# Routes of an expert layer: paired one-hots, row gathers that follow the quads, and route stores in four pieces

## What is computed

```
for l in range(2):
    h = rmsnorm(x, norm1_g[l]) * (1 + sc1) + sh1
    x = x + g1 * hybrid_mixer(h, ...)          # y = sum_i sigmoid(gate_i(h)) * (branch_i @ w_branch[i])
    h = rmsnorm(x, norm2_g[l]) * (1 + sc2) + sh2
    x = x + g2 * peer_ffn(h, ...)

def peer_ffn(h, w_q, sub_keys, u_tab, v_tab):  # 128 x 128 experts, 8 heads, top 16 of each
    experts, g = top16(product keys)           # 128 (expert, share) pairs for each token
    a = gelu(h . u_tab[experts]) * g
    return sum over experts of a * v_tab[experts]
```

## Time and profile before

| what | value |
|---|---|
| median of three runs | 4460.01 us (4444.33 to 4460.23) |
| the profiled execution, its own time | 4453.37 us |
| span of its core | 4451.4 us |
| TensorE, matmul busy | 3973.7 us, 89% |
| VectorE busy | 2640.4 us, 59% |
| ScalarE busy | 1511.7 us, 34% |
| GpSimd busy | 1276.2 us, 29% |
| mean granted TensorE clock | 0.954 |
| DMA | 906.71 MB, mean 204 GB/s |

### The profile page before, as it was taken

The page is one execution under the profiler, slowest core; times in us unless marked ns, Lnnn a source line. Parts: engine busy times, 40 slices in busy tenths (PEclk is TensorE's granted clock), DMA queues, the critical chain, the costliest instruction groups (busy, mean ns, idle before and its releaser), DMA issues.

```text
span 4451.4 us, 61311 instructions
## 1 busy us (share of the span) xinstructions
PE 3973.7 (89%) x18070; PEld 2992.1 (67%) x18070; DVE 2640.4 (59%) x5662; ACT 1511.7 (34%) x2428; POOL 1276.2 (29%) x884
## 2 busy tenths in 40 slices
PE   5888999799998989999869889997999988899998
PEld 2334455399998987777624344653999888777776
DVE  3443323246997957777634432331579988577776
ACT  3224333233443333333332333432334433333332
POOL 0000000046865652222100000000468655422221
PEclk9898999999999999999989899998999999999999
DMA  4341112134788899998634311122357888888885
GB/s 167 114 146 44 56 50 93 69 136 162 262 299 306 339 334 328 327 335 319 217 117 149 104 50 54 62 90 76 136 186 257 315 301 323 323 323 318 321 323 217
DMA packets 340821, 906.71 MB, mean 204 GB/s; under 512 B 28688, under 2 KB 160016, under 8 KB 337168
## 3 DMA queue, kind: packets, MB, share of 16 engines
q1 hardware_dynamic: 215824, 497.43, 31.7%
q0 software_dynamic: 84480, 306.22, 18.6%
q10 hardware_dynamic: 40320, 100.68, 5.9%
HBM read 788.87 MB, written 115.34 MB: 203 GB/s over the span
## 4 chain that ended last, share of the span: by engine, by line
PE 44%; DMA 17%; issue 15%; DVE 15%; POOL 4%; ACT 3%; DVEq 1%; POOLq 0%; SPq 0%; ACTq 0%; PEldq 0%
DMA W<-tab_v 14%; PE bank L683 13%; PE bank L753 7%; PE bank L672 4%; PE bank L674 4%; PE bank L673 4%; DVE u_lo L1950 3%; PE bank L809 2%; PE bank L780 2%; POOL gathered_rows L1431 2%; DMA gathered_rows<-u_rows,arena 2%; PE bank L739 1%; DVE gathered_rows L1820 1%; DVE arena L1860 1%; PE bank L723 1%
## 5 line engine op out<-in xcount | busy, mean ns | idle before, releaser
L1423 POOL TENSOR_TENSOR u_lo<-W,u_hi 128x1024 fp32r<-128x1024 f32 x272 | 688.7, 2533 | 1154.2 <-ACT u_hi L1256 1152.1
L672 PE MATMUL bank<-h_hi,u_hi 128*128 128x384 f32 (+1 forms) x2176 | 765.9, 352 | 48.5 <-POOL u_lo L1423 46.1
L673 PE MATMUL bank<-h_lo,u_hi 128*128 128x384 f32 (+1 forms) x2176 | 744.8, 342 | 0.0
L674 PE MATMUL bank<-h_hi,u_lo 128*128 128x384 f32 (+1 forms) x2176 | 744.6, 342 | 0.0
L672 PE MATMUL bank<-u_hi,a_hi 128*128 128x512 f32 x1536 | 608.7, 396 | 74.3 <-DVE a_lo L1954 74.1
L674 PE MATMUL bank<-u_hi,a_lo 128*128 128x512 f32 x1536 | 604.3, 393 | 0.0
L673 PE MATMUL bank<-u_lo,a_hi 128*128 128x512 f32 x1536 | 604.3, 393 | 0.0
L1339 ACT ACTIVATE u_hi<-W 128x1024 fp32r<-128x1024 f32 x256 | 272.5, 1064 | 756.3 <-DMA W<-tab_v 388.2
L672 PEld LDWEIGHTS bank<-h_hi,u_hi 128*128 128x128 f32 x2176 | 417.3, 192 | 59.7 <-issue 37.0
L673 PEld LDWEIGHTS bank<-h_lo,u_hi 128*128 128x128 f32 x2176 | 417.2, 192 | 5.4
L674 PEld LDWEIGHTS bank<-h_hi,u_lo 128*128 128x128 f32 x2176 | 415.3, 191 | 5.4
(11 more groups left out here) (191 smaller groups left out, 5774.5 us busy)
## 6 DMA issues: line engine op xcount, KB each, us to landing
W<-tab_u SPq DMA_DIRECT2D x256, 512.0 KB, 3.7
W<-tab_v SPq DMA_DIRECT2D x256, 512.0 KB, 9.5
W<-stream SPq DMA_DIRECT2D x206, 512.0 KB, 3.7
act_scratch<-act_out ACTq DMA_DIRECT2D x256, 192.0 KB
route_scratch<-arena ACTq DMA_DIRECT2D x24, 2048.0 KB, 11.1
act_in<-act_scratch SPq DMA_DIRECT2D x64, 768.0 KB, 5.7
g_cur<-route_scratch SPq DMA_DIRECT2D x64, 768.0 KB, 10.2
gate_raw<-gate_tiles POOLq DMA_DIRECT2D x48, 512.0 KB, 4.1
```

Source lines behind the costliest of these rows:

```text
L672: mm(out, w[0], a[0], start=first, stop=False)
L673: mm(out, w[0], a[1], start=False, stop=False)
L674: return mm(out, w[1], a[0], start=False, stop=last)
L1423: nc.gpsimd.tensor_tensor(u_parts[1][:, b, :], raw, u_parts[0][:, b, :].bitcast(F32), ALU.subtract).then_inc(col_lo.sem, 1)
```

## The change

Five edits:
- The two one-hots of a quad lie beside each other in memory and are made by one tensor_tensor of 1024 elements; the share is multiplied in by a second tensor_tensor of 512 elements, in place, after the row product, from a copy of the shares in bank 3. The waits for the picks and the two copies of the shares stand at the head of the stage and at q = 2 of its first step.
- The gathers follow a list, GATHERED: 28 rows plus the quads of the columns so far, at most four in one column, and two a column in "rest".
- A group's store goes out as four transfers of 1024 columns, two in a column of the loop (all that is left at the last), and the semaphore's counts are four times as high.
- The gate products of a turn come directly after its scores, ahead of turn, output and the parts beside.
- Waits on the store's semaphore follow the new counts.

```diff
@@ -311,6 +311,7 @@
 
         at[0] = shared
         route = [carve(128 * TOKENS, [128, TOKENS]) for _ in range(2)]
+        onehots = arena[:, at[0]:at[0] + 4096].rearrange("p (s b t i) -> p s b t i", s=2, b=4, t=4)
         cand = carve(HEADS * 256, [HEADS, 256])
         onehot16 = carve(HEADS * 256, [HEADS * 16, 16])
         pickT = carve(3 * DENSE, [3, DENSE])
@@ -444,12 +445,17 @@
             QUADS[n] = list(range(first, first + width))
             first += width
         assert first == Q, first
+        GATHERED, ahead = [], 24 + 4
+        for c in range(2 * COLUMNS["route"] + COLUMNS["rest"]):
+            ahead += len(QUADS[c % COLUMNS["route"]]) if c < 2 * COLUMNS["route"] else 2
+            GATHERED.append(min(ahead, SPARSE + 6))
         iota_placed = sem("iota_placed")
+        shares_placed = sem("shares_placed")
         onehots_i = signal("onehots_i", {"route": Q})
         onehots_g = signal("onehots_g", {"route": Q})
         route_product = signal("route_product", {"route": Q})
         route_copied = signal("route_copied", {"route": Q})
-        route_stored = [Signal(sem(f"route_stored{b}"), {"route": 48}, credit=16) for b in range(2)]
+        route_stored = [Signal(sem(f"route_stored{b}"), {"route": 192}, credit=16) for b in range(2)]
 
         h_hi_done = sem("h_hi_done")
         h_lo_done = sem("h_lo_done")
@@ -645,7 +651,7 @@
 
 
                 for b in range(2):
-                    sp.wait_ge(route_stored[b].sem, route_stored[b].at("route", layer, STEPS["route"] - 1, 48))
+                    sp.wait_ge(route_stored[b].sem, route_stored[b].at("route", layer, STEPS["route"] - 1, 192))
                     sp.wait_ge(act_stored[b].sem, act_stored[b].at("rest", layer, 0, 0))
                     sp.sem_inc(held, 1)
                 load_down(0, first=True)
@@ -813,6 +819,9 @@
                 for u in range(len(units) + 3):
                     if u < len(units):
                         scores(u)
+                    if stage in GATE_WORK:
+                        for i, k in gate_products(stage, u):
+                            gate_product(stage, layer, step, i, k, bool(beside))
                     if 2 <= u <= len(units) + 1:
                         turn(u - 2)
                         if stage == "swa":
@@ -821,9 +830,6 @@
                         output(u - 3)
                     for part in [p for after, p in beside if after == u]:
                         part()
-                    if stage in GATE_WORK:
-                        for i, k in gate_products(stage, u):
-                            gate_product(stage, layer, step, i, k, bool(beside))
                     if stage == "swa" and u == 0 and not beside:
 
                         load_wait("swa", layer, step, 0)
@@ -1298,6 +1304,8 @@
                     columns("select", 0)
                     with act.Fori(1, TT) as step:
                         columns("select", step, former=step - 1)
+                    unsent = []
+
                     def copy_routes(step, n):
 
                         for q in QUADS[n]:
@@ -1305,15 +1313,23 @@
                             b = group % 2
                             act.wait_ge(route_product.sem, route_product.at("route", layer, step, q + 1))
                             if q % 8 == 0:
-                                act.wait_ge(route_stored[b].sem, route_stored[b].at("route", layer, step, 16 * (group // 2)))
+                                act.wait_ge(route_stored[b].sem, route_stored[b].at("route", layer, step, 64 * (group // 2)))
                             t0 = q % 8 * 4
                             fn(route[b][:, :, t0:t0 + 4], PS[q % 3][:].rearrange("p (t j) -> p j t", t=4), ACT.Copy
                                ).then_inc(route_copied.sem, 1)
                             if q % 8 == 7:
                                 act.wait_ge(route_copied.sem, route_copied.at("route", layer, step, q + 1))
-                                act.dma_start(route_dram[:, ds(step * 6 + group, 1), :].rearrange("p a n -> p (a n)"),
-                                              route[b].rearrange("p j t -> p (j t)")
-                                              ).then_inc(route_stored[b].sem, 16)
+                                unsent.extend((group, part) for part in range(4))
+
+                    def send_routes(step, n):
+
+                        for _ in range(len(unsent) if n == COLUMNS["route"] - 1 else min(2, len(unsent))):
+                            group, part = unsent.pop(0)
+                            b = group % 2
+                            act.dma_start(route_dram[:, ds(step * 6 + group, 1), part * 1024:part * 1024 + 1024
+                                                     ].rearrange("p a n -> p (a n)"),
+                                          route[b][:, 32 * part:32 * part + 32, :].rearrange("p j t -> p (j t)")
+                                          ).then_inc(route_stored[b].sem, 16)
 
                     exponentials(TT - 1)
                     with act.Fori(0, STEPS["route"]) as step:
@@ -1321,6 +1337,7 @@
                             lead("route", step, n)
                             if n >= 2:
                                 copy_routes(step, n - 2)
+                                send_routes(step, n)
                             read_column("route", step, n - 2)
                     for n in range(COLUMNS["rest"]):
                         lead("rest", 0, n)
@@ -1349,7 +1366,7 @@
                         read_column("rest", 0, 6 + n)
 
                     for b in range(2):
-                        act.wait_ge(route_stored[b].sem, route_stored[b].at("route", layer, STEPS["route"] - 1, 48))
+                        act.wait_ge(route_stored[b].sem, route_stored[b].at("route", layer, STEPS["route"] - 1, 192))
                         act.sem_inc(held, 1)
 
                     def splits(step, last=False):
@@ -1451,10 +1468,11 @@
                                 lower("route", c // COLUMNS["route"], c % COLUMNS["route"])
                             else:
                                 lower("rest", 0, c - 2 * COLUMNS["route"])
-                            for _ in range(4 if c == 0 else 2):
-                                if upcoming < SPARSE + 6:
-                                    gather(upcoming)
-                                    upcoming += 1
+                            issued = 0
+                            while upcoming < GATHERED[c] and issued < 4:
+                                gather(upcoming)
+                                upcoming += 1
+                                issued += 1
                         assert upcoming == SPARSE + 6
                         for j in range(KEYS):
                             if upcoming < 2 * SPARSE:
@@ -1888,6 +1906,11 @@
                     for step in range(1, TT):
                         select(step, step - 1 if step > 1 else None, range(8 * (step - 1), 8 * step))
                     dve.wait_ge(iota_placed, layer + 1)
+                    dve.wait_ge(picks_copied.sem, picks_copied.at("picked", layer, 1, 1))
+                    dve.sem_inc(held, 1)
+                    shares = PS[3][:, 128:512]
+                    nc.vector.tensor_copy(shares[:, 0:256], pickT[:, 2, 0:256]).then_inc(shares_placed, 1)
+                    dve.wait_ge(shares_placed, layer * 2 + 1)
                     dve.sem_inc(held, 1)
 
                     for step in range(2):
@@ -1896,20 +1919,22 @@
                                 copy_picks(TT - 1)
                                 dve.wait_ge(picks_copied.sem, picks_copied.at("picked", layer, 2, 1))
                                 dve.sem_inc(held, 1)
-                            elif step == 0 and q == 0:
-                                dve.wait_ge(picks_copied.sem, picks_copied.at("picked", layer, 1, 1))
+                                nc.vector.tensor_copy(shares[:, 256:384], pickT[:, 2, 256:384]).then_inc(shares_placed, 1)
+                                dve.wait_ge(shares_placed, layer * 2 + 2)
                                 dve.sem_inc(held, 1)
 
                             dve.wait_ge(route_product.sem, route_product.at("route", layer, step, q - 3))
                             four = step * (DENSE // 2) + 4 * q
                             iota = PS[3][:, 0:128]
-                            tt(oh_i[:, q % 4], pickT[:, 0, four:four + 4].unsqueeze(2).broadcast_to([128, 4, 128]),
-                               iota.unsqueeze(1).broadcast_to([128, 4, 128]), ALU.is_equal).then_inc(onehots_i.sem, 1)
-                            for t in range(4):
-                                last = ts(oh_g[:, q % 4, t, :], iota, pickT[:, 1, four + t:four + t + 1],
-                                          pickT[:, 2, four + t:four + t + 1], ALU.is_equal, ALU.mult)
-                            last.then_inc(onehots_g.sem, 1)
+                            tt(onehots[:, :, q % 4],
```

(7 more changed lines are left out.)

## The result

| what | before | after |
|---|---|---|
| median, same chip | 4452.17 us (4442.16 to 4460.23, 4 runs) | 4335.07 us (4316.62 to 4342.01, 4 runs) |
| ratio, 95% interval | | 0.9732 [0.9698, 0.9765] |
| the profiled execution, its own time | 4453.37 us | 4316.62 us |
| span of its core | 4451.4 us | 4315.1 us |
| mean granted TensorE clock | 0.954 | 0.965 |

The change is faster by 2.7%, 31 us under the forecast of 4366 us: inside the range of 4325 to 4425, and at the lower end of the forecast's own 4335 to 4395. The kernel before has one run more here than ahead, hence its other median. The granted clock is given as a share of 2.4 GHz.

A forecast was written before the change was run, and what follows sets the result against it. Route stages: TensorE, VectorE and DMA close together, VectorE setting the pace and waiting for rows. At 305 us a layer they gain 77.8, "rest" 4, gates 7: 88.8 from 4453.4 is 4364.6, stated as 4366 us, range 4325 to 4425.

The forecast's parts named there:

- The rows: Route stages: issuing gathers by quad count nearly ends VectorE's waits for gathered rows, 44.8 and at least 45.1 us a layer.
- All eight buffers stay filled: Route gathers: a row is reissued when the one eight before is used, giving 20 us for landings of at most 13.6.
- I add 7.6 us for meeting them unevenly: Route stage: DMA engines and TensorE both full at about 297 us, so 7.6 us a layer added, making 305.
- the turn: Between the two steps of a route stage: ScalarE stands for 6.8 us, counted as 5.5 us a layer, not shortened.
- the floor of 285.6: Route stage: TensorE's own matmul time a layer, from 36, 8 and 4 columns with two, three and no quads.
- Rival B: Route stages: DMA traffic binds harder, at 349 GB/s; 318 us a layer, gain 63, whole 4390 us; chance 0.18.
- The pair: Route one-hots on VectorE: compare 1.14 plus multiply 0.60, 1.74 against 1.88 us, so a quad costs 2.88 us.
- rival C: Route stages: new VectorE forms run at the slow in-place multiply rate, 4.42 us a quad; slower, 4603 us; chance 0.06.
- One quad less of cover: Route, VectorE: the multiply queues behind a row's landing, so a late row holds its own quad, not the next; unpriced.
- The stores: Route, ScalarE's queue: four 512 KB pieces free small stores and gathers from standing behind 2 MB; 9 us more engine time.
- The gates: Mixers swa and mla: gate products moved ahead of turn and output gain 3.5 us a layer, 7 in all, between -5 and +18.
- "Rest", 2 us a layer: "Rest" columns: the eight late rows are issued earlier, shortening ScalarE's 4.7 us wait; 2 us a layer, 4 in all.

The follow-up runs named there:

- the last version: Changed kernel with one store a group and ScalarE's rounding of the next step's first tile moved ahead of the turn; median 4319.23 us, ratio 0.9714.

## Why the prediction came out so

**The rows: right, in mechanism and size.** The two stages were to gain 34.5 and 43.3 us; they gained 38.2 and 46.5, and the list alone 33.7 and 42.7. In the second layer the good fit owes something to chance, as both figures count from an execution with a long stage. The waits went to zero and 0.5 us. "All eight buffers stay filled" was too much: a freed buffer waits 5.0 us in the median for its next gather (2.8 with the list alone). That GpSimd issues column by column, so that a freed buffer waits for the next split, would explain it; no run tested that. With it the lead is 16.1 us where I counted 20 (19.5 with the list alone), still above the landings of before.

**"I add 7.6 us for meeting them unevenly": not there.** The engines are busy 0.96 of the stage and TensorE waits for no tile but at the turn. What stands above the floor of 285.6 is 15.7 us, and it can be read off the distances between TensorE's columns: 2 in the first two columns, 4 in the four three-quad columns of the first step (7.8 to 7.9 us against 6.84), 9 at the turn (columns 22, 23 and 24 take 4.8, 10.3 and 8.2 us against 4.16, 4.16 and 5.95), and 1 in the last two. I had 2.3, 3 and 5.5 for the first three of them and 1 for the shares: the turn was mis-sized by 3.5 us, because I took ScalarE's stall for the whole loss, and not what follows it, a table load, the split, and a column partly at the slow clock. The trace of before had it: its columns 22, 23 and 24 take 4.3, 9.5 and 8.0 us, 7.5 in all above the floor. The two misses cancel in part (305 against 301.5), which is luck. Rival B falls.

**The pair: sizes right, one term missing.** 1.13 and 0.60 us for 1.14 and 0.60, 2.87 us a quad for 2.88; rival C falls. "One quad less of cover" was named and given no price: a term put at nothing without a reason. Its price is 55 us when rows are late, and doesn't show when they are in time: the change is only sound as a whole. I saw the term and did not ask what it would do in the kernel of before, where the row waits were at hand.

**The stores: the gain didn't come, nor did the cost.** "ScalarE's small stores and the gathers no longer stand behind 2 MB": with the pieces alone the rows are still waited for 42.1 us. The 9 us of engine time were at most 3. "Two in a column (under 1 us)" missed the last column, with four issues in 2.92 us. How long a piece takes to land the trace does not give. The estimate by the Trainium skill ("DMA: Bandwidth & Descriptors", "Anatomy of one DMA"), 12.8 us for four pieces one behind the other against 6.8, can't be tested here, since the pieces leave in two columns and lie beside other traffic (and that fit is for transfers issued by GpSimd, where these are ScalarE's); that batching to a MiB or more matters ("Measured") is not borne out in this stage: 2.51 and 2.47 us a MB with whole stores, 2.52 and 2.55 with quarters.

**The gates: the step that failed.** Predicted 7 us and allowed -5 to +18, measured 37; this alone takes the time from the forecast to the edge of its own range. "The wait of the turn for the scaled probabilities, 2.4 us in mla, now has gate products ahead of it" picked the wait by the stage that I had opened, and left out swa, which the hunk touches as well. There the 12.1 us of waits for the rotation stood in one row of the waits view. I also priced a wait at its own length; behind it TensorE ran at the lower clock, and 9.3 us of swa's gain are busy time. The risk (a gate product that meets its bank too early) was small where it showed, 2.4 us in swa; mla got some 4 us shorter a layer. What I said of the end of a stage, 1 us, is there at the entry of fox.

**"Rest", 2 us a layer:** 2.6 and 1.7, but kernels without the list take 39.1 to 45.5 us there and those with it 38.7 to 40.7, so a single pair of executions does not show it. **Sum:** 84.7 + 4.3 + 35.6 for 77.8 + 4 + 7, and 10.4 in "down", which no edit reaches: 135 us between the two profiled executions (136.8 in their own times), 117 between the medians. So the profiled run flatters the change by some 20 us, and the medians carry the verdict.

## What to carry to other kernels

Give a producer that feeds a queue of buffers the consumer's own count (rows used so far), not an average per column. Never put work that others wait for behind a wait for a transfer: the same pair was worth 11 us with the transfers in time and cost 55 with late ones, and moving its multiply ahead of the row product removed the loss. And look for a filler's best place by the longest chain that it can cover, counted from where the chain begins, in every stage that the loop serves.

## What the hardware showed that was not expected

- **Traffic at 0.96 of the DMA engines didn't hold TensorE up.** 366 GB/s over 302 us, and 370 in the last version (296 us), with no wait of TensorE for a tile outside the turn. The Trainium skill ("DMA: Bandwidth & Descriptors", "Specifications") puts a core's share of HBM at about 358; the one core that runs here stays above it for whole stages.
- **The turn of the route loop costs ScalarE 4.8 to 7.6 us, whatever comes next.** That is the span over the kernels here: 5.5 and 5.8 in the change, 6.8 and 7.2 before. It held back the rounding of a tile, and held back the gelu when the rounding stood ahead of it; the 12-column "select" loop shows no such stall. By the Trainium skill ("Runtime: NRT & Kernel Launch", "Instruction fetch mechanics") a taken branch out of the pages at hand makes the engine fetch its code by a DMA first. The long body with a stall and the short one without agree with that. So do the queues that the profile calls instruction, which move three packets in 1389:1396 of after, where the stall lies, though the trace does not say for which engine. No run here tested it.
- **A wait costs its length and the clock behind it.** Behind the 2.83 us wait four gate matmuls took 3.42 us instead of 1.88, at a granted clock of 0.54, and in swa 5.2 us less waiting for the rotation (3.7 us less idle time in all) came with 9.3 us less busy time for the same products.
